# Seven quarter products in place of eight for the gate and up projections of a two-block transformer kernel, two pairs of weight pieces at a time

## What is computed

```python
# first block
h = rms_norm(x, norm_mlp[layer])
x = x + jnp.square(jax.nn.relu(h @ w_up[layer])) @ w_down[layer]        # 1024 -> 4096 -> 1024

# second block, twice a layer, two layers (D_FF_2 = 2816)
mod = (c_act @ w_ada[l] + b_ada[l]).reshape(B, N_MOD, D_MODEL)          # c_act = silu(c)
h = modulate(rms_norm_2(x, norm_gain[l, 0]), mod[:, 0], mod[:, 1])
x = x + 0.5 * mod[:, 2][:, None, :] * swiglu(h, w_gate, w_up, w_down)

def swiglu(h, w_gate, w_up, w_down):
    return (jax.nn.silu(h @ w_gate) * (h @ w_up)) @ w_down
```

## Time and profile before

| what | value |
|---|---|
| median of 3 runs | 3502.74 us (3502.47 to 3504.43) |
| profiled execution, first to last instruction | 3498.8 us |
| TensorE busy | 3407.7 us, 97% |
| VectorE, ScalarE, GpSimd busy | 34%, 25%, 68% |
| mean granted TensorE clock | 0.993 |

### The profile page before, as it was taken

The page is one execution under the profiler, slowest core; times in us unless marked ns, Lnnn a source line. Parts: engine busy times, 40 slices in busy tenths (PEclk is TensorE's granted clock), DMA queues, the critical chain, the costliest instruction groups (busy, mean ns, idle before and its releaser), DMA issues.

```text
span 3498.8 us, 42521 instructions
## 1 busy us (share of the span) xinstructions
PE 3407.7 (97%) x17034; PEld 2738.7 (78%) x17034; DVE 1179.6 (34%) x2514; ACT 885.8 (25%) x1876; POOL 2369.8 (68%) x1242
## 2 busy tenths in 40 slices
PE   8888999999999999999999999999999999999999
PEld 6655777988898888667779888888887677798887
DVE  6554332433443234442223111332244422241111
ACT  2656551211120102354312000210012543221000
POOL 7515447787778776645677877687775546678775
PEclk9999999999999999999999999999999999999999
DMA  3222213444535442212232222254432122223222
GB/s 142 68 69 82 67 62 108 149 171 170 185 127 204 168 166 94 73 58 85 85 106 96 97 97 96 83 220 165 171 126 73 67 76 79 82 97 106 98 98 73
DMA packets 104773, 388.09 MB, mean 111 GB/s; under 512 B 12017, under 2 KB 12401, under 8 KB 98433
## 3 DMA queue, kind: packets, MB, share of 16 engines
q1 hardware_dynamic: 88272, 292.76, 24.4%
q10 hardware_dynamic: 16304, 92.62, 7.0%
HBM read 383.20 MB, written 2.13 MB: 110 GB/s over the span
## 4 chain that ended last, share of the span: by engine, by line
PE 92%; DVE 4%; ACT 3%; issue 1%; ACTq 0%; DVEq 0%
PE psum L1234 28%; PE psum L1236 27%; PE psum L1235 27%; PE psum L1307 2%; PE psum L1349 2%; PE psum L1324 2%; PE psum L1293 1%; DVE rs_t L1695 1%; ACT s_sb L1477 0%; DVE s_sb L1736 0%; ACT L1477 0%; ACT s_sb L1495 0%; PE psum L1407 0%; PE psum L1285 0%; DVE n_sum L1906 0%
## 5 line engine op out<-in xcount | busy, mean ns | idle before, releaser
L1202 POOL TENSOR_TENSOR w_hi<-raw,ones 128x1024 fp32r<-128x1024 f32 (+2 forms) x593 | 1041.3, 1756 | 990.4 <-PE psum L1236 981.2
L1205 POOL TENSOR_TENSOR w_lo<-raw,w_hi 128x1024 fp32r<-128x1024 f32 (+2 forms) x593 | 1315.1, 2218 | 46.5
L1234 PE MATMUL psum<-h_hi,w_hi 128*128 128x512 f32 (+2 forms) x2912 | 1143.4, 393 | 19.4 <-DVE r L1711 9.4
L1236 PE MATMUL psum<-h_hi,w_lo 128*128 128x512 f32 (+2 forms) x2912 | 1105.3, 380 | 0.0
L1235 PE MATMUL psum<-h_lo,w_hi 128*128 128x512 f32 (+2 forms) x2912 | 1104.8, 379 | 0.0
L1234 PEld LDWEIGHTS psum<-h_hi,w_hi 128*128 128x128 f32 (+1 forms) x2912 | 550.2, 189 | 156.6 <-issue 35.9
L1236 PEld LDWEIGHTS psum<-h_hi,w_lo 128*128 128x128 f32 (+1 forms) x2912 | 549.7, 189 | 106.6
L1235 PEld LDWEIGHTS psum<-h_lo,w_hi 128*128 128x128 f32 (+1 forms) x2912 | 550.9, 189 | 103.3 <-issue 9.0
L1234 PE MATMUL psum<-a_hi,w_hi 128*128 128x512 f32 (+1 forms) x1064 | 392.5, 369 | 0.0
L1235 PE MATMUL psum<-a_lo,w_hi 128*128 128x512 f32 (+1 forms) x1064 | 391.8, 368 | 0.0
L1236 PE MATMUL psum<-a_hi,w_lo 128*128 128x512 f32 (+1 forms) x1064 | 391.8, 368 | 0.0
(11 more groups left out here) (198 smaller groups left out, 3299.5 us busy)
## 6 DMA issues: line engine op xcount, KB each, us to landing
raw<-weights_dram SPq DMA_DIRECT2D x487, 512.0 KB, 3.3
ada_t<-ada_dram ACTq DMA_DIRECT2D x48, 1536.0 KB, 7.1
raw<-weights_dram SPq DMA_DIRECT2D x76, 256.0 KB, 2.6
raw<-weights_dram SPq DMA_DIRECT2D x32, 384.0 KB, 2.9
bias_t<-biases_dram ACTq DMA_DIRECT2D x36, 256.0 KB, 2.9
bias_t<-cum_dram ACTq DMA_DIRECT2D x16, 256.0 KB, 3.9
out_dram<-x SPq DMA_DIRECT2D x8, 256.0 KB, 2.1
raw<-weights_dram SPq DMA_DIRECT2D x4, 408.0 KB, 3.1
```

What stands on the lines that cost most here:

```text
L1202: nc.gpsimd.tensor_tensor(high, piece, ones[:, 0:1].to_broadcast([P, n]), ALU.mult)\
L1205: nc.gpsimd.tensor_tensor(w_lo[:, p % NR, 0:n], piece, high.bitcast(F32), ALU.subtract)\
L1234: mm(dst, lh, rh, start=first, stop=False)
L1236: return mm(dst, ll, rh, start=False, stop=last)
```

## The change

All gate and up groups but the first ones after a norm are taken in pairs of weight pieces, and two pairs make a set: gates of tiles t and t+1, then ups of the same tiles (in the MLP ups t, t+1 and ups t+2, t+3). With W (1024 by 256, a pair) and h (1024 by 512 tokens) each cut in four quarters, a pair is computed by Winograd's form of Strassen's product: seven products of quarters (P1 to P7) in place of eight. A product is 4 chunks by 3 matmuls of 256 columns, 12 matmuls. The seven run in the order P1, P2, P6, P5, P7, P3, P4. What it adds:

- four sums of quarters of W per pair on VectorE (`first_sums`, `last_sum`), in place in `raw` and in `s2`
- the high part of each of the seven quarter operands on ScalarE (`operand_high`), 128x512; the low part on GpSimd (`low`), that of P3 on VectorE. The ring `w_hi` still has six places; a place now holds a quarter operand's high and low part
- per pair three copies of half banks on ScalarE (`keep`), three additions on half banks on VectorE (`combine`)
- per norm four steps of sums of h (`quarter_sum`, four instructions of 128x256 each on VectorE), their high parts on ScalarE and low parts (128x1024) on VectorE. The scaled norm `n_out` now lies in SBUF instead of PSUM
- four groups in halves after a norm instead of three; 47 sets in all (7 in the MLP, 10 in each of four feed-forwards)
- `c` in SBUF (`c_t`) instead of PSUM; two sums to a load instead of three

```diff
-ADA = 3
+ADA = 2
+SET_BANKS = (((0, 1), (2, 3)), ((6, 7), (5, 4)))
+QUARTER = KC // 2 * P
+PRODUCTS = ("P1", "P2", "P6", "P5", "P7", "P3", "P4")
+LOW_BY = dict(P3="dve")
...
+def new_set(kinds, slots, banks, norm, ffn=True):
...
+    for p in pairs:
+        for what in PRODUCTS:
+            assert tick("product_done") == p.ops[what].n
+            put("product", p.ops[what])
+            if what == "P1":
+                p.p1 = tick("copied")
+                put("keep", p, "P1")
+            elif what == "P2":
+                p.c11 = tick("combined")
+                put("c11", p)
+            elif what == "P6":
+                p.u2 = tick("copied")
+                put("keep", p, "P6")
+            elif what == "P5":
+                p.p5 = tick("copied")
+                put("keep", p, "P5")
+            elif what == "P7":
+                p.c22 = tick("combined")
+                put("c22", p)
+            elif what == "P4":
+                result(p, 1)
+            elif what == "P3":
+                p.c12 = tick("combined")
+                put("c12", p)
+                result(p, 0)
...
+def with_operands():
...
+        while place < len(RING) and (place < NH or place - NH in free):
+            one = RING[place]
+            needed = [one] if isinstance(one, int) else one.pair.pieces
+            if any(p >= NR and p - NR not in gone for p in needed):
+                return
+            yield "operand", one
...
+    for step in ORDER:
+        yield step
...
+        elif step[0] == "product":
+            free.add(step[1].place)
+        yield from ready()
...
+            def product(op):
+                pair, what, m = op.pair, op.what, op.pair.norm
+                E.wait_at(op.low)
...
+                elif what == "P6":
+                    E.wait_ge("copied", pair.p1)
+                elif what == "P5":
+                    E.wait_ge("combined", pair.c11)
+                elif what == "P7":
+                    E.wait_ge("copied", pair.u2)
+                elif what == "P4":
+                    E.wait_ge("combined", pair.c22)
+                elif what == "P3":
+                    E.wait_ge("copied", pair.p5)
...
+                        E.wait_ge("t_lo", m.sums + k + 1)
...
+            def operand_high(op):
+                if op.place >= NH:
+                    E.wait_at(freed(op.place))
+                src, ready = source_of(op)
+                E.wait_at(ready)
+                fn(high_of(op), src, ACT.Copy).then_inc(sem["operand_hi"], 1)
...
+            def first_sums(pair):
...
+                E.wait_at(pair.ops["P1"].low)
+                E.wait_ge(f"loaded{q % NR}", 16 * (q // NR + 1))
+                v.tensor_tensor(a, a, c, ALU.subtract).then_inc(sem["sums_made"], 1)
+                E.wait_ge("sums_made", made + 1)
+                v.tensor_tensor(s2[pair.side][:], d, a, ALU.subtract).then_inc(sem["sums_made"], 1)
+                v.tensor_tensor(c, c, d, ALU.add).then_inc(sem["sums_made"], 1)
...
-                    ins = v.tensor_tensor_reduce(out=part, in0=part, in1=c_bcast, scale=1.0, scalar=0.0, op0=ALU.mult,
+                    ins = v.tensor_tensor_reduce(out=part, in0=part, in1=c_t[:], scale=1.0, scalar=0.0, op0=ALU.mult,
```

398 lines of the change are left out of this document (328 added, 70 removed).

## The result

The changed kernel takes 3918.4 us against 3502.6 us: ratio 1.1185, 95% interval 1.1167 to 1.1202, slower by 416 us. The forecast was 3703 with a range up to 3790. The sign was right, the size was not. The profiled run that came with the result stood at a granted clock of 0.649 throughout, so I read the profile of a repeat of the same kernel (3917.7 us).

What follows compares the result with a forecast made beforehand. TensorE, 97% busy, was taken to bound the kernel; -75 + 2 + 101 + 50 + 58 + 10 + 54 = +200 on 3502.7 gave 3703 us. The forecast's own range was 3640 to 3770, the wider one 3570 to 3790.

Steps and rivals of the forecast that it cites:

- gain of 94 pairs, fourth group: Gates and ups on TensorE: 94 pairs each 0.80 us shorter, -75 us; the fourth group in halves after norms, +2.
- wait ahead of P3: P3 waits for the copy of P5, behind the next pair's P6 high part on ScalarE: 78 x 1.3, +101 us.
- wait ahead of P6, modulation sums between sets: P6 in a set's first pair waits for the copy of P1, +50 us; modulation sums at 14 places between sets, +58.
- modulation sums between `down` groups: GpSimd needs 6.1 us per `down` group against 5.44 but is two pieces ahead: 7 stretches at 1.5, +10 us.
- norm: After norms the first P6 waits for sums of h, and TensorE 2 us for `x`: 14.8 + 4 x 9.7, +54 us.
- (3): VectorE-GpSimd exclusion bites harder: first weight sum loses 0.7 us more per pair, `down` groups cost 39; 3798 us, chance 0.10.
- (2): VectorE-GpSimd exclusion does not bite, P3 waits only 0.35 us: +107, 3610 us; chance 0.17 with what lies down to 3570.
- (1): Faster: ScalarE reaches the two copies in time, so waits ahead of P3 and P6 vanish; 3478 us, chance 0.13.
- (4): Whole kernel: nothing gained, nothing lost, the waits sum to 75 us; no mechanism of its own, chance 0.02.

Runs made afterwards that it cites:

- n1_copy: all7 with sets only in the second feed-forwards (16), and on ScalarE the copy of P1 ahead of the previous set's last high part: 3508.8 us, ratio 1.0020.
- sums_late: Changed kernel with VectorE's weight sums among `down` groups put two additions to `x` later: 3837.0 us.
- ada_narrow: Changed kernel with modulation sums taken over 2 columns instead of 1024, so the modulation is not computed in full: 3822.6 us.
- c_psum: Changed kernel with nearly all modulation sums moved between `down` groups, there reading a copy of `c` in two PSUM banks: 3820.6 us.
- fill_down: Changed kernel with 492 unneeded matmuls of 512 columns in the waits ahead of the sixth `down` group of each of eleven runs: 3905.8 us.
- keepfirst: Changed kernel with a ring place given back behind the copy or addition of its product, not ahead of it: 3881.8 us.
- ring8: Changed kernel with eight places for quarter operands instead of six: 4005.0 us.
- ring8_keep: ring8 with the order of keepfirst, copies and additions ahead of the operands: 3885.7 us.
- all5: ring8_keep with the edits of sums_late and c_psum, and the next pair's first weight sums behind the addition after P2: 3649.2 us.
- all7: all5 with four more plain groups after each norm, and on ScalarE the next P6's operand behind the copies of P6 and P5: 3604.4 us.
- p4_first: Changed kernel with P4 ahead of P3 again, all else the same: 3961.5 us.

## Why the prediction was wrong, point by point

The 416 us divide so. Waits are TensorE's idle time in the trace, clock is half of its working time at the lower level.

| step of the prediction | forecast | measured |
|---|---|---|
| gain of 94 pairs, fourth group | -73 | -73 taken |
| wait ahead of P3 | 101 | 71.6 (56 waits) |
| wait ahead of P6, modulation sums between sets | 108 | 125.7 (P6 101.3, P5 22.1, P4 2.3) |
| modulation sums between `down` groups | 10 | 113.2, of which 64.2 stay with narrow sums |
| norm | 44 ahead of P6, 10 ahead of the first halves | 52.3, 27.5 (30.2 less the 2.7 of before) |
| clock | 0 | 77.0 |
| rest | 0 | 22 |

Of the 216 us that the forecast lacked, 103 are the `down` groups, 77 the clock, 26 the norm, 18 the waits ahead of P6 and P5, and 22 the rest; the waits ahead of P3 give 30 back.

**The gain** stands as taken; the trace shows matmuls 0.120 apart, and n1_copy a set of 21.39, which is 20.16 and 1.2 of waits and starts.

**P3** was right in mechanism and size, 1.22 to 1.29 in 54 of 56 for 1.3, and wrong in number: 56 places for 78. The 22 others are 14 pairs whose P6 waits for modulation sums, the five after norms, and three whose P5 waits: there the copy of P5 is in time. The step "The wait ahead of P3" added waits that exclude each other.

**P6** was right: 1.08 in the feed-forwards for 1.15, 1.69 in the MLP for 1.8, 4.67 at most modulation steps for 3.4 + 1.15. At the last step of a stage the wait stands ahead of P5 instead, 5.8 us in the MLP and 8.2 in each layer, where two steps meet; these 22.1 us are more than the whole difference of 18.

**The `down` groups** are the step that failed most, 10 us for 113.2, and the sentence is "Between `down` groups GpSimd needs 1.74 + 2.24 + 2 x 1.07 = 6.1 per group against 5.44, but is two pieces ahead". The two numbers are right; with modulation sums between, GpSimd's low parts start 6.17 us apart (740.97, 747.14). What I left out is who waits. By the prices GpSimd is not ahead when a run begins (worked out, no view shows it by itself): the last six products give six places back in 8.6 us, each for a piece that takes it 4.3. It catches up by 1.1 a group, and with modulation sums falls back by 0.7. TensorE does not need it sooner, but the next set's weight sums do, and behind those, on VectorE, stands an addition to `x`. I had that row before my eyes, at the norm ("The first weight sums stand ahead of the last addition to `x`"), and charged it there at 2 us (measured 5.3 to 6.1) and at the eleven like places hardly. sums_late (-81 us) shows that this order is the cause, and ada_narrow and c_psum (13.1 to 5.8) what the modulation sums add to it.

**The norm** inside the first P6 came out 9 us above its 44, by the chain forecast; only the copy of P1, behind the last high part of the sums of h, stood in for the last chunk.

**The clock** was not in the sum: a term put at nothing without a reason, and measured at 77 us. The 0.993 of before was taken as fixed; it became 0.955. fill_down shows for one kind of wait that it is a price of standing still.

**The rest** is the start after a wait: a matmul's record lasts 0.28 us where the next would start after 0.12, so 0.16 or more at each of 125 more waits is in no idle column: 20 us of the 22. By the 0.23 of a set it would be 29, so this term is an estimate.

**Rivals.** (3) was the nearest in number, 3798, by luck: its main term, 66 us for the first weight sum, did not come (L2006 took over 0.7 us in 12 of 94 cases), and its 39 at the `down` groups is the slowing of GpSimd alone (49 by ada_narrow), not the order behind it. (2) is out: the second sum's median is 1.66 us. (1) and (4) are out by the waits that stand:

```profile
L2006 DVE TENSOR_TENSOR raw<-raw x94: 680/693/1736, 660.1 to 3862.2; 128x512 f32<-128x512 f32 x94
L2008 DVE TENSOR_TENSOR s<-raw x94: 691/1664/1673, 660.8 to 3862.9; 128x512 f32<-128x512 f32 x94
```

## What to carry to other kernels

When work for a later stage is put ahead in an in-order queue, price each instruction behind it, in every stage where it can land, not only where the new work is used. Removing one wait of such a ring mostly shows the next one: of seven edits of order and lead (keepfirst, sums_late, ring8, ring8_keep, all5, all7, n1_copy) six gave back less than the wait they aimed at, and one cost 87 us. A forecast that comes out in sum may still have the wrong parts, as p4_first did. A saving of 7% on a product is small beside one stall of 13 us in it, and an estimate for an engine that will stand still needs a term for its clock.

## What the runs showed of the hardware that I had not expected

- A modulation sum on VectorE that takes 1.22 us alone, and GpSimd's 2.40 and 1.90, become 3.41, 3.26 and 2.87 when they take turns, in this timeline of the changed kernel. With `c` in PSUM the sum took 1.208 to 1.223 in all 136 cases.

```profile
740.97 3.26 POOL L1414 TENSOR_TENSOR w_lo<-raw,w_hi 128x1024 fp32r<-128x1024 f32 x1
...
741.90 3.41 DVE L2192 CUSTOM_DVE_ANT_0 ada_t<-ada_t,c_t 128x1024 f32<-128x1024 f32 x1
...
744.19 2.87 POOL L1411 TENSOR_TENSOR w_hi<-raw,ones 128x1024 fp32r<-128x1024 f32 x1
```

- 492 more matmuls in the waits made the kernel 12 us faster.
- Putting P4 ahead of P3 added 4 us of idle time and 33 us of lost pace: the same sets ran at a granted clock of 0.97 and not 1.00.
- The first matmul after a wait is followed by the next after 0.20 us, not 0.12 (2279.01, 2279.21).
